# A22's low part in twelve pairs of block products: made by VectorE instead of an accumulating transfer

## The reference

```python
def _mlp(x, g, w_up, w_down):
    h = _rmsnorm(x, g)
    return jnp.square(jax.nn.relu(h @ w_up)) @ w_down
```

## Time and profile before

| what | us |
|---|---|
| median of 3 runs | 940.68 |
| the profiled execution, device time | 939.73 |
| its span, first to last instruction | 938.0 |
| TensorE busy (matmul) | 925.6 |
| VectorE busy | 654.8 |
| ScalarE busy | 587.7 |
| POOL busy | 229.9 |

### The profile page before, as it was taken

The page is one execution under the profiler, slowest core; times in us unless marked ns, Lnnn a source line. Parts: engine busy times, 40 slices in busy tenths (PEclk is TensorE's granted clock), DMA queues, the critical chain, the costliest instruction groups (busy, mean ns, idle before and its releaser), DMA issues.

```text
span 938.0 us, 19495 instructions
## 1 busy us (share of the span) xinstructions
PE 925.6 (99%) x7329; PEld 905.5 (97%) x7329; DVE 654.8 (70%) x1181; ACT 587.7 (63%) x980; POOL 229.9 (25%) x200
## 2 busy tenths in 40 slices
PE   8999999999999999999999999999999999999997
PEld 8999999999999999999999999999999999999997
DVE  6579999999999999998563335873488258722233
ACT  6787887878787878776833445653465356523353
POOL 5311010101010110101243443223422431244440
PEclk9999999999999999999999999999999999999999
DMA  7777667675858484859232233386238534852202
GB/s 183 156 175 136 171 126 179 118 186 104 180 113 192 101 196 99 172 131 208 60 111 80 81 89 90 92 177 161 68 95 183 150 90 90 191 134 87 85 23 96
DMA packets 194716, 120.95 MB, mean 129 GB/s; under 512 B 36014, under 2 KB 181854, under 8 KB 194667
## 3 DMA queue, kind: packets, MB, share of 16 engines
q1 hardware_dynamic: 176666, 80.28, 31.7%
q0 software_dynamic: 12816, 37.23, 22.3%
q10 hardware_dynamic: 5184, 2.78, 1.1%
HBM read 75.97 MB, written 7.06 MB: 89 GB/s over the span
## 4 chain that ended last, share of the span: by engine, by line
PE 92%; DMA 3%; ACT 2%; DVE 1%; POOL 1%; issue 1%; ACTq 0%; DVEq 0%
PE dense L661 67%; PE z L983 6%; PE dense L983 4%; PE z L781 3%; PE dense L955 3%; DMA w_lo<-w_raw 2%; PE z L745 2%; PE z L815 2%; POOL w_lo L614 1%; PE z L661 1%; DMA x_tok<-in_x_sample_dram 1%; PE z L749 1%; PE dense L825 0%; ACT n L1090 0%; PE z L947 0%
## 5 line engine op out<-in xcount | busy, mean ns | idle before, releaser
L661 PE MATMUL dense<-r_hi,w_hi 128*128 128x272 f32 (+1 forms) x1008 | 210.6, 291 | 1.4 <-ACT r_hi L1118 0.7
L661 PE MATMUL dense<-r_lo,w_hi 128*128 128x272 f32 (+1 forms) x1008 | 209.6, 289 | 0.0
L661 PE MATMUL dense<-r_hi,w_lo 128*128 128x272 f32 (+1 forms) x1008 | 209.5, 289 | 0.0
L632 POOL TENSOR_TENSOR w_lo<-w_raw,w_hi 128x1024 fp32r<-128x1024 f32 x56 | 134.6, 2409 | 197.3 <-ACT w_hi L1072 197.3
L1562 DVE SCALAR_TENSOR_TENSOR acc<-conv_in,cw_cur,acc 128x574 f32<-128x574 f32 x232 | 172.8, 811 | 0.5
L661 PEld LDWEIGHTS dense<-r_hi,w_hi 128*128 128x128 f32 x1008 | 158.2, 188 | 1.9 <-issue 0.9
L661 PEld LDWEIGHTS dense<-r_lo,w_hi 128*128 128x128 f32 x1008 | 158.7, 188 | 0.6 <-DVE r_lo L1543 0.6
L661 PEld LDWEIGHTS dense<-r_hi,w_lo 128*128 128x128 f32 x1008 | 159.0, 188 | 0.0
L1072 ACT ACTIVATE w_hi<-w_raw 128x1024 fp32r<-128x1024 f32 x110 | 115.3, 1052 | 34.0 <-PE z L983 22.0
L609 POOL DMA_DIRECT2D w_lo<-w_raw x53 | 45.1, 851 | 361.2 <-ACT w_lo L1074 361.2
L661 PE MATMUL dense<-s_hi,w_hi 128*128 128x272 f32 x640 | 132.2, 288 | 0.0
(11 more groups left out here) (301 smaller groups left out, 1913.3 us busy)
## 6 DMA issues: line engine op xcount, KB each, us to landing
w_raw<-in_w_in_dram SPq DMA_DIRECT2D x54, 512.0 KB, 5.5
w_lo<-w_raw POOLq DMA_DIRECT2D x53, 512.0 KB, 5.1
w_raw<-in_w_up_dram SPq DMA_DIRECT2D x32, 512.0 KB, 4.2
w_raw<-in_w_down_dram SPq DMA_DIRECT2D x32, 512.0 KB, 3.9
w_lo<-w_raw POOLq DMA_DIRECT2D x36, 256.0 KB, 4.7
w_raw<-in_w_pw_dram SPq DMA_DIRECT2D x8, 512.0 KB, 4.0
w_raw<-in_w_out_dram SPq DMA_DIRECT2D x8, 512.0 KB, 3.9
x_tok<-in_x_prompt_dram SPq DMA_DIRECT2D x4, 512.0 KB, 6.3
```

The lines of the kernel that those rows point to most:

```text
L632: pool.tensor_tensor(w_lo[:, n], w_raw[:, n], w_hi[:, n].bitcast(F32), ALU.subtract).then_inc(lo_post, 1)
L661: mm = nc.tensor.matmul(out[:, h, 0:half], w[:, wslot, k, :], m[:, k, c0 + h * half:c0 + (h + 1) * half], start=(k == 0 and n == 0), stop= ...
```

## The change

A22 is taken out of `BY_DMA`. ScalarE no longer writes the negated copy of A22, POOL no longer issues a transfer for it, and VectorE subtracts the high part from the raw quarter instead, in all twelve pairs. In the first pair of a round this stands at the end of the up part's last unit, in the other pairs directly behind `x11`. Whoever waits for A22's low part (TensorE and SyncE) now waits for VectorE's signal, which counts by 1. The helpers `by_dma`, `low_signal` and `low_wait` only name this.

```diff
-        BY_DMA = ("A11", "A12", "A22")
+        BY_DMA = ("A11", "A12")
...
+        def low_signal(P_, name):
+            return wform_lo[MADE[name] - 1], 1
+
+        def low_wait(P_, name):
+            return wform_lo[MADE[name] - 1], (16 if name in BY_DMA else 1) * (P_ + 1)
...
         def low_made(engine, P_, name):
-            engine.wait_ge(wform_lo[MADE[name] - 1], (16 if name in BY_DMA else 1) * (P_ + 1))
+            engine.wait_ge(*low_wait(P_, name))
...
                     u_low(rr, m, "B22", b22)
                     u_low(rr, m, "T4", usum("T4"))
+                    if f == KC - 1:
+                        wsum_low(PAIRS * rr, "A22")
...
             def wsum_low(P_, name):
-                if name not in BY_DMA:
+                if not by_dma(P_, name):
                     dve.wait_ge(wform_hi, PRODUCTS * P_ + MADE[name])
-                    nc.vector.tensor_tensor(form_place(w_lo, name), wsum(name), form_place(w_hi, name).bitcast(F32), ALU.subtract).then_inc(wform_lo[MADE[name] - 1], 1)
+                    nc.vector.tensor_tensor(form_place(w_lo, name), raw_form(P_, name), form_place(w_hi, name).bitcast(F32), ALU.subtract).then_inc(*low_signal(P_, name))
...
                 else:
                     made(P_, "A11")
                     add_product(P_, "x11")
+                    wsum_low(P_, "A22")
                     if p == 1:
                         wsum_low(P_, "S3")
                         wsum_low(P_, "S4")
```

More of the change, by code:

```diff
@@ L337, in build, with by_dma @@
                  ("S3", "T3", 0, False), ("S4", "B22", 1, False), ("A22", "T4", 0, False))
+        def by_dma(P_, name):
+            return name in BY_DMA
+        def low_signal(P_, name):
+            return wform_lo[MADE[name] - 1], 1
+        def low_wait(P_, name):
+            return wform_lo[MADE[name] - 1], (16 if name in BY_DMA else 1) * (P_ + 1)
         def low_made(engine, P_, name):
-            engine.wait_ge(wform_lo[MADE[name] - 1], (16 if name in BY_DMA else 1) * (P_ + 1))
+            engine.wait_ge(*low_wait(P_, name))
         MADE = {w: n + 1 for n, (w, _, _, _) in enumerate(SEVEN)}
@@ L634, in seven_low @@
             def seven_low(P_):
-                for name in BY_DMA:
+                for name in [name for name in BY_DMA if by_dma(P_, name)]:
                     pool.wait_ge(wform_hi, PRODUCTS * P_ + MADE[name])
@@ L1386, in form_high @@
                     mm = nc.scalar.activation(form_place(w_hi, name), raw_form(P_, name), ACT.Copy)
-                    if name in BY_DMA:
+                    if by_dma(P_, name):
                         mm = nc.scalar.activation(form_place(w_lo, name), raw_form(P_, name), ACT.Copy, scale=-1.0)
```

## The result

The changed kernel takes 944.81 us, the median of 6 runs (943.69 to 946.62); the kernel before took 941.00 beside it (6 runs, 939.51 to 943.46). The ratio is 1.0045, 95% interval 1.0035 to 1.0055: 4.2 us slower (3.3 to 5.2). Forecast was 944.2.

What follows compares the result with a forecast made beforehand. TensorE, busy 99% of the span, bounds the kernel, so only its idle spots count. Second-pair delays 1.11 - 0.68 + 1.56 + 1.56 = +3.55 us on the median of 940.68 gave 944.2, range 940.2 to 946.6.

Steps and rivals of the forecast that it cites:

- The path: TensorE's second pair: the fifth product starts 0.58 after VectorE starts `x12`, so a later `x12` delays everything behind it.
- The load that starts with A11's transfer: Second pair: SyncE's earlier 512 KB load starts beside A11's transfer, which then takes 5.5 us instead of 3.2 alone.
- L: Time of A11's second-pair transfer from issue to landing with a load beside it: 5.5 us taken, bounds 3.2 and 7.2.
- VectorE's 0.60 in the second pair: A22's added subtraction behind `x11` steps 0.60 with nothing to cover it, delaying `x12` by that much.
- A22's high part behind those of S3 and S4: Second pair: VectorE must wait for ScalarE's high part of A22, ready at 616.39 in round one, 708.86 in round two.
- the second case: Rival: the load does not hold up A11, only VectorE's 0.60 counts in second pairs: +0.7, 941.4; chance 0.26.
- The waits for A22: TensorE's stops for A22's accumulating transfer in first pairs and round one's second pair, together 3.4 us, go.
- Round one's 0.48 in the second pair: TensorE's wait for A22 in round one's second pair, 0.48 lost, is got back.
- 0.2 in the third: TensorE's stall of 0.2 at the third pair's fifth product in round one goes.
- The sum: Second-pair delays of 1.11, 1.56 and 1.56 by round, less 0.68 in round one: +3.55 us net, 944.2.
- the prediction's formula: Net change as 3L - 12.95 for L above about 4.55; below it +0.7.

Runs made afterwards that it cites:

- e5: Changed kernel, but VectorE makes A22's low part only in each round's first pair, elsewhere copy and transfer as before: 941.88 against 941.19 us, ratio 1.0015.
- e2: Changed kernel, but SyncE issues the load of the third pair's second block only when A11's transfer has landed: 941.04 against 940.33 us, ratio 1.0009.
- e4: Changed kernel with the load held until A11's transfer landed and A22's subtraction behind `x12` in the second pair: 937.17 against 940.33 us, ratio 0.9966.
- e8: Changed kernel, A22's subtraction behind `x12` in the second pair, load issued when the first pair's `x22` is added: 936.73 against 941.19 us, ratio 0.9953.
- e3: Changed kernel, but in each round's second pair A22's subtraction stands behind `x12` instead of `x11`: 942.65 against 940.33 us, ratio 1.0024.
- e7: Changed kernel with A22's subtraction made twice in each round's second pair: 945.61 against 941.19 us, ratio 1.0053.
- e6: Changed kernel, but A22's low part by transfer in each round's first pair, by VectorE in the second to fourth: 943.37 against 941.19 us, ratio 1.0022.
- e1: The changed kernel again, unaltered, beside the kernel before on one chip: 944.53 against 940.33 us, ratio 1.0040.
- the first experiments: The four experiments e1 to e4, measured on one chip beside the kernel before, which took 940.33 us there (22 runs).

## Why the prediction was right

**The path.** TensorE's stops were the thing to follow. In all ten profiles the second pair's `x12` starts 0.58 to 0.59 in front of the fifth product, in every round but two. Those two are the rounds in which the clock had fallen (round three of the changed kernel, round two of e5); there it starts 1.0 and 1.1 in front, and TensorE doesn't wait for it.

**The load that starts with A11's transfer.** This was the larger term, read from three transfers elsewhere in the same trace. L was put at 5.5; the fifteen of the five profiles in which the load is issued with A11's transfer, at most 0.02 us later, took 5.25 to 5.78. Held back or 1.45 later it is 3.3 to 3.7 (e2, e4, e8), and the time follows.

**VectorE's 0.60 in the second pair.** It steps 0.60; moved away it gives back 0.6 in each round (e3), and made twice it costs 0.72 more, what the second one steps (e7).

**A22's high part behind those of S3 and S4.** The prediction had it as what decides once A11 is on time, at 616.39 in round one, that is 0.9 after `x11` would end. e2 shows that wait, 0.91, and its time lies 0.7 over before, the value of the second case.

**The waits for A22.** All went, as forecast. Those of the first pairs were worth nothing, since `x12` of the second pair was not earlier; in e4 and e8, where it is, they are won. Round one's 0.48 in the second pair and 0.2 in the third lie behind that `x12` and were won in the changed kernel too, as the sum had it.

**The sum.** By rounds +0.43, +1.56, +1.56; measured +0.39, +1.31, +2.46 in the first profile and +0.46, +1.32, +1.48 in the second. Round two's was 0.25 high: L was 5.3 there, and I had left out a gap of 0.07 in the third pair that went too. Round three's was 0.9 low in the first profile: 0.3 for an L of 5.78, and 0.6 for the slow clock, for which the sum had no term. With the three L's of the first profile the prediction's formula gives 3.75, with those of the second 3.47; measured are 4.16 and 3.26. The ratio's 4.2 us (3.3 to 5.2) holds the sum of 3.55. That the median comes within 0.7 of it is in part luck: L was taken from two transfers of the first pairs, which took 5.4 to 6.5 in rounds two and three over the ten profiles, and 6.8 to 7.7 in round one. In every experiment the time by the ratio and the sum of the profile's three stretches agree to within 1 us, about the ratios' own uncertainty. Why the part in front of them varies by 2.9 us was not tried.

**Not tried:** why two transfers that start together take so long. The rows show when, not in which part of the path. Nor was it tried why A11's transfer took 5.29 in round one of e6. The queues' view has a 16 KB packet of the instruction queue in that stretch and none in the same stretch of rounds two and three; whether it is the cause is open.

## What to carry to other kernels

When a low part, or any small result, comes earlier, look at every waiter of it, the load queue too: here SyncE took the earlier signal and put a 512 KB load on top of the one transfer that TensorE needed next. The remedy was not to undo the change but to start the load 1.4 us later and to move one of the subtractions. And an instruction that waits for a later task of another engine should not stand in front of work that is ready: A22 belongs behind `x12`.

## What the runs showed of the hardware

An accumulating transfer of 256 KB takes 3.2 us alone, 3.7 with a 512 KB load issued 1.45 later (e8), and 5.25 to 5.78 with one issued within 0.02 us (second pairs of five profiles). So there 1.4 us between the two issues decide over 1.6 to 2.1 us. The distance alone doesn't tell all: in e6, with another transfer 1.0 in front and a load 2.3 behind, it took 4.04 in rounds two and three and 5.29 in round one.

After a stop of about 2 us TensorE's clock can fall to the 1.2 GHz level for 3.4 us, 0.5 to 1.2 us after it resumed. The granted clock is 0.50 or 0.51 there. It isn't certain: of fifteen stops of 1.7 to 2.3 us in five profiles (the changed kernel twice, e3, e5, e7) two were followed by it, one of 2.3 and one of 2.0, and one of 2.1 was not. Of the changed kernel's first six executions four have a mean granted clock of 0.995 or 0.996 and take 944.5 to 946.6 us, two have 0.999 and take 943.7 and 944.0; all 22 of the kernel before beside the first experiments have 0.997 to 0.999. Fifteen matmuls took 1.5 us more each time, of which 0.6 and 1.3 were lost and the rest took the place of a later wait (1 to 1.6 were expected before e1). So it is a part of the price of a stop.
